# Second layer: four of eight key tiles moved between the pieces of compression and linear attention

## The reference, cut to what matters

```
o_gla = gla_mixer(...)        # linear attention, chunks of 64, decays exp(b_t - b_s)
o_nsa = nsa_mixer(...)        # compressed keys/values (gelu(blocks @ w1) @ w2) + windowed attention
h = h + concat([o_gla, o_nsa]) @ w_out
h = h + cross_attn(rms_norm(h), rms_norm(mem), wq, wk, wv, wo)   # k = memn @ wk, v = memn @ wv
```

## Time and profile before

| | |
|---|---|
| median of 3 executions | 2052.94 us (2052.8 to 2053.95) |
| the profiled execution, its own time | 2054.33 us |
| its span | 2052.6 us |
| mean granted TensorE clock | 0.962 |
| TensorE busy | 1941.6 us (95%) |
| VectorE busy | 1381.4 us (67%) |
| ScalarE busy | 1164.0 us (57%) |

### The profile page before, as it was taken

The page is one execution under the profiler, slowest core; times in us unless marked ns, Lnnn a source line. Parts: engine busy times, 40 slices in busy tenths (PEclk is TensorE's granted clock), DMA queues, the critical chain, the costliest instruction groups (busy, mean ns, idle before and its releaser), DMA issues. The chain is left out here.

```text
span 2052.6 us, 29416 instructions
## 1 busy us (share of the span) xinstructions
PE 1941.6 (95%) x11449; PEld 1666.9 (81%) x11449; DVE 1381.4 (67%) x1837; ACT 1164.0 (57%) x1850; POOL 5.5 (0%) x25
## 2 busy tenths in 40 slices
PE   7998789999999998899999899998999999999998
PEld 6987478888888886489865859998999998888886
DVE  3662389999999996325351435998888885666665
ACT  3451279999999995324142324443577774444454
POOL 1000000000000000000000000000000000000000
PEclk9999889999999999999789998999999999999999
DMA  8434349999999998434212012554544345555553
GB/s 327 165 124 137 123 184 377 378 376 373 377 376 375 376 385 353 158 124 157 69 42 91 33 62 74 185 184 151 184 138 134 131 133 191 194 194 195 195 192 136
DMA packets 84960, 418.32 MB, mean 204 GB/s; under 512 B 14091, under 2 KB 16592, under 8 KB 51930
## 3 DMA queue, kind: packets, MB, share of 16 engines
q1 hardware_dynamic: 74592, 406.98, 54.3%
q10 hardware_dynamic: 10234, 9.48, 1.6%
HBM read 415.36 MB, written 1.06 MB: 203 GB/s over the span
## 5 line engine op out<-in xcount | busy, mean ns | idle before, releaser
L2139 DVE TENSOR_TENSOR slot_lo<-arena,w_hi 128x2048 fp32r<-128x2048 f32 x192 | 433.7, 2287 | 23.4 <-ACT w_hi L1578 21.9
L2497 DVE TENSOR_TENSOR tab_lo<-arena,tab_hi 128x1024 fp32r<-128x1024 f32 x256 | 312.6, 1225 | 125.8 <-ACT tab_hi L1917 123.7
L1578 ACT CAST w_hi<-arena 128x2048 fp32r<-128x2048 f32 x192 | 363.3, 1917 | 8.3 <-PE bank L1034 8.1
L1917 ACT CAST tab_hi<-arena 128x1024 fp32r<-128x1024 f32 x256 | 267.4, 1045 | 0.2
L1460 PE MATMUL bank<-x_hi,tab_lo 128*128 128x256 f32 x1024 | 144.2, 284 | 7.9 <-DVE tab_lo L2497 7.9
L1460 PE MATMUL bank<-x_hi,tab_hi 128*128 128x256 f32 x1024 | 149.1, 289 | 2.0 <-ACT tab_hi L1917 2.0
L1951 ACT CAST e_hi<-arena 128x256 fp32r<-128x256 f32 x128 | 52.0, 407 | 173.7 <-PE bank L1493 172.9
L1030 PE MATMUL bank<-w_hi,gathP 128*128 128x512 f32 x512 | 139.6, 395 | 5.5 <-ACT gathP L1599 5.5
L1924 ACT ACTIVATE arena<-bank 128x256 f32<-128x256 f32 (+16 forms) x128 | 43.7, 342 | 174.6 <-PE bank L1460 174.6
L1460 PE MATMUL bank<-nT_lo,tab_hi 128*128 128x256 f32 x1024 | 142.3, 280 | 0.0
L1034 PE MATMUL bank<-slot_lo,gathP 128*128 128x512 f32 x512 | 138.4, 392 | 0.4 <-DVE slot_lo L2139 0.4
(11 more groups left out here) (402 smaller groups left out, 3218.5 us busy)
## 6 DMA issues: line engine op xcount, KB each, us to landing
arena<-in_w_dram SPq DMA_DIRECT2D x192, 1024.0 KB, 9.9
arena<-in_peer_down_dram SPq DMA_DIRECT2D x128, 512.0 KB, 3.3
arena<-in_peer_up_dram SPq DMA_DIRECT2D x128, 512.0 KB, 3.3
arena<-in_packed_later_dram SPq DMA_DIRECT2D x36, 1024.0 KB, 7.1
arena<-in_packed_first_dram SPq DMA_DIRECT2D x28, 1024.0 KB, 7.3
arena<-in_packed_later_dram SPq DMA_DIRECT2D x2, 816.0 KB, 11.6
arena<-in_packed_later_dram SPq DMA_DIRECT2D x2, 768.0 KB, 8.7
h<-in_x_dram ACTq DMA_DIRECT2D x1, 1024.0 KB, 5.0
```

The costliest lines, as they stand in the source:

```text
L1578: nc.scalar.copy(hi_of(e, g), portion_of(slot, e, g)).then_inc(S("w_hi"), 1)
L1917: nc.scalar.copy(tab_hi[n % HI][:, :], tab[n % PR]).then_inc(S("table_hi"), 1)
L2139: nc.vector.tensor_tensor(portion_of(slot_lo, e, g), portion_of(slot, e, g), hi_of(e, g).bitcast(F32), ALU.subtract).then_inc(S("w_lo"), 1)
L2497: nc.vector.tensor_tensor(tab_lo[n % PR][:, :], tab[n % PR], tab_hi[n % HI][:, :].bitcast(F32), ALU.subtract).then_inc(S("table_lo"), 1)
```

## The change

Key tiles 0 to 3 stay where they are. Key tiles 4 to 7 move behind `gla_far`, `cmp_hidden`, `gla_near` and `cmp_out`, one behind each. They use banks 2 and 3 instead of the ring of banks 4 to 7. Tiles 6 and 7 wait until tiles 4 and 5 have been read, and `gla_blocks(1)`, which uses banks 2 and 3 too, waits until tile 7 has been read. `cmp_hidden`, which uses bank 4, waits for the reading of tile 3 only. On ScalarE the copies of tiles 5, 6 and 7 move accordingly. The arithmetic is the same.

```diff
-            if tag[0] == "mem" and tag[1] >= KT:
-                return bank[6 + tag[1] % 2]
+            if tag[0] == "mem" and tag[1] >= KT // 2:
+                return bank[(6 if tag[1] >= KT else 2) + tag[1] % 2]
...
+            def key_tile(c):
+                if c < KT // 2:
+                    b = tile_bank(pe, ("mem", c))
+                else:
+                    tile_no["mem", c] = len(tile_no)
+                    if c >= KT // 2 + 2:
+                        pe.wait_ge(S("tile_read"), tile_no["mem", c - 2] + 1)
+                    b = bank[2 + c % 2]
+                mem_part(c, b, range(KT))
+
             pe.wait_ge(S("mem_normed"), 1)
-            for c in range(KT):
-                mem_part(c, tile_bank(pe, ("mem", c)), range(KT))
+            for c in range(KT // 2):
+                key_tile(c)
...
             def cmp_hidden():
                 pe.wait_ge(S("cmp_w1_in"), 32)
-                pe.wait_ge(S("tile_read"), tile_no["mem", KT - 1] + 1)
+                pe.wait_ge(S("tile_read"), tile_no["mem", KT // 2 - 1] + 1)
...
             pe.wait_ge(S("cmp_in_ready"), 2)
             gla_far()
+            key_tile(4)
             cmp_hidden()
+            key_tile(5)
             gla_near()
+            key_tile(6)
             cmp_out()
+            key_tile(7)
+            pe.wait_ge(S("tile_read"), tile_no["mem", KT - 1] + 1)
             gla_blocks(1)
             gla_blocks(2)
...
             q_exp(2)
-            for c in range(3, KT):
-                read_mem(c)
+            read_mem(3)
+            read_mem(4)
             act.wait_ge(S("cmp_hidden"), 1)
...
                     S("gla_far_copied"), 1)
+            read_mem(5)
             act.dma_start(bias_sw[:, :, :], toeplitz(table_dram, T - P + 1, 1, P, HEADS, TAB, T)).then_inc(S("bias2_in"), 16)
+            read_mem(6)
             act.wait_ge(S("cmp_out"), 1)
             nc.scalar.copy(k_cmpT[:, :], bank[5][:, 0:2 * N_CMP])
             k_exp(2)
+            read_mem(7)
```

## The result

The changed kernel takes 2056.93 us (median of 12 runs, 2055.57 to 2058.66) against 2052.70 (12 runs, 2051.90 to 2053.97) for the kernel before: a ratio of 1.0021, 95% interval 1.0012 to 1.0030, so 2.5 to 6.2 us slower. Measured once more on another occasion it came to 2056.86 against 2052.43, 1.0020 (1.0011 to 1.0029). The forecast was 2058.6, in a range of 2053.5 to 2062.0.

A forecast was written before the change was run, and what follows sets the result against it. TensorE, busy 1941.6 of 2052.6 us, was taken to set the end in most stages. The terms +3.4 + 1.7 + 0 + 2.2 + 0.5 - 0.9 - 1.2 = +5.7 us on the 2052.94 median gave 2058.6 us, range 2053.5 to 2062.0.

The forecast's parts named there:

- rival B: The wait alone: no clock fall behind it, or its cost given back in `cmp_hidden` and `gla_blocks(2)`; +3.0 us, chance 0.21.
- A: The forecast itself: a new wait and key tiles at half clock, +5.7 us, chance 0.65.
- Steps 1, 6 and 7: New wait ahead of `gla_far` +3.4 us; reading of tile 7 ahead of `gla_blocks(1)` +0.5; wait for `k_product(2)` gone -0.9.
- Step 2: Behind the new wait, `gla_far` and key tile 4 run partly at half clock: +1.7 us, bounds 0 and 3.5.
- Step 3: `cmp_hidden` stays at 11.64 us behind dense work: 0, with a saving of about 3 us named as possible.
- rival C: Key tiles between the short matmuls hold the clock up, making the kernel faster: -6.8 us, chance 0.06.
- Step 4: Key tile 5 comes into the half-clock stretch behind `cmp_hidden`: +2.2 us, bounds 0 and 3.6.
- Step 8: `gla_blocks(2)`, now nearer to dense work, runs partly at full clock: -1.2 us, bounds 0 and -2.5.
- Step 9: Products with the values 0, though up to 2.7 us gain possible; first value halves as cold as before, 0, bounds +-1.8.
- third sign of being wrong: The prediction is wrong if the lag is smaller at 1100 us than at the end of `gla_blocks(2)`.
- D: The delay is taken back in TensorE's waits for VectorE at the windowed attention's start: about +1 us, chance 0.08.

The follow-up runs named there:

- e1: Against the changed kernel: all eight key tiles ahead of `gla_far` again, keeping its banks and extra waits; 2052.07 us, 0.9996 of the kernel before.
- e4: Changed kernel plus eight matmuls with unused result in the wait ahead of `gla_far`; 2053.53 us, 1.0000 of the kernel before.
- e3: Changed kernel with key tile 5 behind `gla_near` instead of between `cmp_hidden` and `gla_near`; 2056.10 us, 1.0015 of the kernel before.
- e5: Against the changed kernel: key tiles 4 to 7 together behind `gla_far`, none between the later pieces; 2056.68 us, 1.0019 of the kernel before.
- e2: Changed kernel with key tile 4 ahead of `gla_far`, so five tiles ahead; 2055.26 us, 1.0013 of the kernel before.
- e6: Against the changed kernel: key tiles 0 to 5 ahead of `gla_far`, 6 behind `gla_near`, 7 behind `cmp_out`; 2052.52 us, 1.0001 of the kernel before.
- e10: As e8, but tile 6 in two halves ahead of the transposes behind the products with the values; 2046.69 us, 0.9970 of the kernel before.
- e12: The kernel of e8 measured once more; 2046.03 us, 0.9969 of the kernel before.
- e8: Against the changed kernel: six tiles ahead of `gla_far`, tile 6 behind `cmp_out`, tile 7 in halves in the windowed attention; 2046.57 us, 0.9977 of the kernel before.
- e7: Against the changed kernel: six tiles ahead of `gla_far`, tile 6 behind `cmp_out`, tile 7 behind `gla_blocks(2)`; 2053.84 us, 1.0004 of the kernel before.
- e9: Against the changed kernel: tiles 0 to 6 ahead of `gla_far`, only tile 7 moved, in halves, to the windowed attention; 2049.57 us, 0.9983 of the kernel before.
- e11: The changed kernel measured once more, on the chip of the last experiments; 2056.86 us, 1.0020 of the kernel before.

## Why the prediction was right, step by step

The sign and the place were right, and the size was near, 5.7 us forecast, 4.2 measured. The nearness is partly luck: two terms were off by 1.7 and 3.5 us and nearly cancelled. The interval of the medians, 2.5 to 6.2 us, holds the +3.0 of rival B as well as the +5.7 of A, so what tells them apart is the profiles and the experiments. The steps of the stage, forecast and measured (start to start, kernel after less kernel before):

| step | forecast | measured |
|---|---|---|
| 1 wait ahead of `gla_far` | +3.4 | +3.5 (971.74 - 954.37 - 27.73 / 2) |
| 2 half clock on `gla_far` and tile 4 | +1.7 | +3.4 (0.77 + 2.61) |
| 3 `cmp_hidden` | 0 | -3.5 |
| 4 tile 5 at half clock | +2.2 | +2.4 |
| 5 tiles 6 and 7, `gla_near`, `cmp_out` | 0 | +0.2 |
| 6 reading of tile 7 | +0.5 | +0.5 |
| 7 wait for `k_product(2)` | -0.9 | -0.9 |
| 8 `gla_blocks` | -1.2 | -0.9 |
| sum at the products | +5.7 | +4.7 |
| 9 products, up to the attention's start | 0 | +0.5 (5.14 - 4.67) |
| 9 attention's start to the second value half | 0 | -0.8 (4.31 - 5.14) |

**Steps 1, 6 and 7** held to 0.1 us. They are waits whose ends could be read off VectorE's and ScalarE's timelines before, and the change didn't move them. e1 shows that nothing of the cost comes from the banks.

**Step 2** had the right mechanism and half the size. The clock stayed at half for 6.8 us, as in the first of the two rows, not 3.4. That row had 2.3 us idle of its 3.41, the other, which the prediction took, 1.0 us idle of 3.42 (not "most" of it); the new wait of 3.4 us was nearer to the first. "Dense work follows at once" didn't shorten it. e4 shows that it is the idle time that costs this. Without it `gla_far` and tile 4 run at full clock at the same position. The page "TensorE: Matmul & The Clock Gate" of the Trainium skill (section "HAM oscillation — how this bites in real kernels") has the burst behind a wait start throttled. By that rule a wait without a clock price was the weaker reading, and the trace sides with it in the price. In the details the row differs: `gla_far` still began at full clock and the fall came at 972.8 us, 1.0 us behind its start, to last until 0.9 us before the end of tile 4.

**Step 3** is the term that was mis-sized: 0 forecast, -3.5 us measured. It also brought one of the prediction's own signs of being wrong, "if `cmp_hidden` runs mostly at full clock": it ran 5.9 of its 8.14 us there. The prediction had named a saving of about 3 us as possible, but entered it neither in the sum nor in its bounds. "`cmp_hidden` stays 11.64 us ... behind dense work, as before" overlooked what stands directly ahead of it: before, that is `gla_far` with its short matmuls, and after, key tile 4. The prediction named the 1.9 us of `gla_far` only against rival C, and gave them no weight. In the five profiles with a key tile directly ahead (the change and its repetition, e3, e4, e5) it takes 8.0 to 8.2 us, in the nine with `gla_far` directly ahead (before, e1, e2, e6 to e10, e12) 10.5 to 11.6. The pair e4 and e6, at the same position to 0.1 us, rules out the idle time and the position as causes. Two profiles of one kernel differ by less, 10.5 and 11.4 us in e8 and e12. The errors of steps 2 and 3, +1.7 and -3.5, are together -1.8 at the products; the small ones of the other steps add up to +0.8, which leaves the forecast 1.0 us too high there. No run has a key tile directly ahead of `cmp_hidden` without either the wait or unused matmuls, so what that order alone would bring stays untested.

**Step 4** held, and e3 and e2 support it: tile 5 takes 5.9 us behind `cmp_hidden` with or without the wait, and full-clock time behind `gla_near`, which takes 7.4 to 7.5 us at either place.

**Step 8** was right in size here, but it isn't firm: without the wait for `k_product(2)` the two `gla_blocks` took 7.3 us in the change, e2 and e4, 7.7 in e12, 8.05 in e3, e6 and e7, and 6.0 in the fastest execution of e8.

**Step 9 and the line to the end.** The delay wasn't the same everywhere behind `gla_blocks(2)`: +4.7 us at the products, +5.1 at the attention's start, +4.3 from the second value half on, since the first one ran at half clock for less of its time (3.36 against 3.78 us). So the third sign of being wrong, a smaller lag at 1100 us, came true too, by 0.4 us.

**Rivals.** B (+3.0) had two branches. The first, that the clock doesn't fall behind the wait, is refuted by the rows above and by e4. The second, that what it costs is given back in `cmp_hidden` and `gla_blocks(2)`, is what happened: +3.4 behind the wait, -3.5 and -0.9 there. What B lacked is the +2.4 of key tile 5. The course of the clock thus lies between A and B, and A's number was the nearer one at the products (4.67 against 5.7 and 3.0), while the medians (4.2) favour neither. C (tiles between the pieces hold the clock up) had more in it than it was given: "one tile can't do what eight didn't" is refuted by e4, where one tile directly ahead kept `cmp_hidden` at full clock for 5.9 us and saved 3.3 against e6. It didn't decide, since the wait and its clock price (+6.8 in e5) came with it, and e6 shows that tiles 6 and 7 between the pieces are worth nothing that can be measured. But e9, e10 and e12 show that key tiles can pay at another place. D (the delay taken back) failed but for those 0.4 us: the weights of the cross-attention are first touched 3.8 us later than before, and 3.8 us is also the difference of the spans. The row of ScalarE's timeline after:

```profile
1101.52 3.70 ACT L790 CAST w_hi<-arena 128x2048 fp32r<-128x2048 f32 x2 [0.24 <-ACTq L479]
```

## What to carry to other kernels

Before work is moved off the place where it covers a wait, read when the covered inputs become ready: here five of the eight tiles were cover, and only the last three could go without a new wait (e2). Price the idle time twice, once for itself and once for the half clock behind it (here 3.5 and 3.4 us), and look which piece will stand in a half-clock stretch, and what stands directly ahead of a piece with few columns: `gla_near` could stand at half clock for 0.1 us, a key tile couldn't, and a key tile ahead of `cmp_hidden` was worth 3.3 to 3.5 us. Look then for a place where TensorE waits for another engine over and over, as at the start of the attention: tile 7 alone moved there gave -2.9 us, with tile 6 moved behind `cmp_out` as well -6.4, where four tiles between the pieces gave +4.2.

## What the runs showed of the hardware

`gla_near`, 16 float32 matmuls with 64 rows and 256 columns each, takes 7.4 to 7.5 us whether it stands at half or at full clock: 7.53 with 4.4 of them at half before, 7.42 all at full in the change. A piece that isn't sped up by the clock is a good one to leave in a slow stretch.

The clock fell under matmuls of 30 columns without any idle time: in e6 TensorE was busy 2.60 of 2.60 us at full clock, and then 8.84 of 8.84 at half. How far into such a piece it fell went with what stood directly ahead (2.6 and 5.9 us, e6 and e4).

Useless matmuls in a wait of 3.4 us made a kernel 3.4 us faster (e4 against the change). Where the clock changes is alike from one execution of a kernel to the next, but not always: in the repetition of the change (e11) every piece is within 0.2 us of its first profile, while e8 and e12, one kernel, differ by 0.9 us in `cmp_hidden` and 1.7 in `gla_blocks`. A difference of 1 to 2 us between two profiles isn't proof of anything by itself.
